# Order and place of small products on TensorE's array, in a two-layer hybrid encoder on one core

## The reference

```python
def retention_mixer(p, cos, sin):
    ...
    scores = jnp.einsum('bcqhd,bcshd->bchqs', q, k) * decay_mask
    o_inner = jnp.einsum('bchqs,bcshe->bcqhe', scores, v)
    ...
    o_cross = jnp.einsum('bcqhd,hq,bchde->bcqhe', q.astype(jnp.float32), q_decay, prev)
    o = (o_inner.astype(jnp.float32) + o_cross).reshape(B, -1, H, d)[:, pad:]

def rwkv7_mixer(p, v_first, vres, mu, w0, w_up, a0, a_up, g_up, k_k, k_a, r_k, gn_w, gn_b):
    ...
    w = w0 + jnp.tanh(wd) @ w_up                 # rank 32
    a = jax.nn.sigmoid(a0 + ad @ a_up)           # rank 32
    g = jax.nn.sigmoid(gd) @ g_up                # rank 64
    if vres is not None:                         # layer 1 only, rank 32
        v = v + (v_first - v) * jax.nn.sigmoid(v0 + (v @ v_down) @ v_up)
    ...
    def step(S, inp):                            # state S of 64 x 64 per head
        sa = jnp.einsum('bhvk,bhk->bhv', S, -kk_t)
        S = (S * w_t[:, :, None, :] + sa[..., None] * (kk_t * a_t)[:, :, None, :]
             + v_t[..., None] * k_t[:, :, None, :])
        return S, jnp.einsum('bhvk,bhk->bhv', S, r_t)
    ...
    y = group_norm_per_head(y); return (y + bonus) * g
```

## Time and profile before

| | |
|---|---|
| median of 3 runs | 3283.07 us |
| profiled execution, its time | 3285.28 us |
| profiled execution, its span | 3283.1 us |
| TensorE matmul busy | 3237.2 us (99%) |
| VectorE busy | 1343.1 us (41%) |
| ScalarE busy | 870.8 us (27%) |
| share of 16 DMA engines' span, weights' queue | 40.0% |
| mean granted TensorE clock | 0.998 |

### The profile page before, as it was taken

How to read it: one execution, slowest core, us unless ns; L and a number is a source line. 1 busy time by engine, 2 the same in 40 slices (tenths; PEclk the granted TensorE clock), 3 DMA queues, 4 the chain that set the end, 5 groups by cost and what they waited for, 6 DMA issues and landing times.

```text
span 3283.1 us, 51407 instructions
## 1 busy us (share of the span) xinstructions
PE 3237.2 (99%) x21648; PEld 2737.6 (83%) x21648; DVE 1343.1 (41%) x3184; ACT 870.8 (27%) x2565; POOL 34.2 (1%) x47
## 2 busy tenths in 40 slices
PE   8999999999999999999999999999999999999998
PEld 6788788888888888878888888888888888888887
DVE  4335451345514454153541544415354154442541
ACT  3323430224303242032430324204232042411320
POOL 0000000000000000000000000000000000000000
PEclk9999999999999999999999999999999999999999
DMA  6233234442444334443334433444334433345443
GB/s 202 70 120 123 97 123 145 145 134 98 135 151 148 126 101 145 154 135 123 109 117 152 138 128 98 148 151 138 118 119 151 159 130 116 123 149 165 149 154 115
DMA packets 128867, 434.79 MB, mean 132 GB/s; under 512 B 13296, under 2 KB 25712, under 8 KB 128384
## 3 DMA queue, kind: packets, MB, share of 16 engines
q1 hardware_dynamic: 127488, 427.32, 40.0%
q0 software_dynamic: 1152, 4.19, 0.3%
HBM read 427.27 MB, written 4.19 MB: 131 GB/s over the span
## 4 chain that ended last, share of the span: by engine, by line
PE 97%; DVE 1%; ACT 1%; issue 0%; DMA 0%; SPq 0%; POOL 0%; ACTq 0%; DVEq 0%
PE psum L859 66%; PE psum L1307 19%; PE psum L853 2%; PE psum L873 2%; PE psum L1107 1%; PE psum L1120 1%; PE psum L1064 1%; PE psum L1123 1%; PE psum L1140 1%; PE psum L1249 1%; PE psum L1232 0%; PE psum L1202 0%; PE psum L1205 0%; PE psum L1187 0%; DMA con<-in_consts 0%
## 5 line engine op out<-in xcount | busy, mean ns | idle before, releaser
L859 PE MATMUL psum<-hT,slots 128*128 128x256 f32 (+2 forms) x8832 | 1998.7, 384 | 10.7 <-DMA con<-in_consts 2.9
L859 PEld LDWEIGHTS psum<-hT,slots 128*128 128x128 f32 x8832 | 1661.4, 190 | 284.4 <-issue 38.6
L1307 PE MATMUL psum<-gT,slots 128*128 128x256 f32 (+1 forms) x2816 | 615.4, 381 | 0.3 <-DVE hT L1411 0.2
L1307 PEld LDWEIGHTS psum<-gT,slots 128*128 128x128 f32 x2816 | 533.9, 190 | 78.5 <-issue 0.5
L1411 DVE SCALAR_TENSOR_TENSOR hT<-hT,psum 128x256 f32<-128x256 f32 (+2 forms) x128 | 54.2, 424 | 617.4 <-PE psum L1307 504.8
L785 ACT ACTIVATE last<-psum 128x2 f32<-128x2 f32 x352 | 60.2, 171 | 904.3 <-PE psum L859 904.2
L859 PE MATMUL psum<-mixT,slots 128*128 128x256 f32 (+2 forms) x1024 | 227.1, 382 | 2.0 <-DVE hT L1411 1.7
L859 PEld LDWEIGHTS psum<-mixT,slots 128*128 128x128 f32 x1024 | 193.6, 190 | 34.3 <-issue 6.6
L1867 DVE TENSOR_SCALAR tmpG<-raw,par 128x256 f32<-128x256 f32 (+2 forms) x176 | 62.5, 355 | 380.0 <-ACT raw L786 379.7
L555 ACT ACTIVATE scr<-hT 128x256 f32<-128x256 f32 (+2 forms) x120 | 47.6, 419 | 587.8 <-DVE hT L1430 564.4
L1867 DVE TENSOR_SCALAR gT<-raw,par 128x256 f32<-128x256 f32 (+2 forms) x176 | 62.3, 354 | 327.5 <-ACT raw L786 327.4
(11 more groups left out here) (246 smaller groups left out, 2386.4 us busy)
## 6 DMA issues: line engine op xcount, KB each, us to landing
slots<-in_weights SPq DMA_DIRECT2D x792, 512.0 KB, 3.4
hT<-in_x SPq DMA_DIRECT2D x8, 512.0 KB, 5.4
out<-prpt POOLq DMA_DIRECT2D x8, 512.0 KB, 3.0
tab<-in_tables SPq DMA_DIRECT2D x6, 512.0 KB, 5.2
con<-in_consts SPq DMA_DIRECT2D x1, 1562.0 KB, 10.6
tab<-in_tables SPq DMA_DIRECT2D x2, 544.0 KB, 5.2
mixT<-in_ln_rows SPq DMA_DIRECT2D x1, 1024.0 KB, 7.0
par<-in_params SPq DMA_DIRECT2D x2, 386.5 KB, 5.5
```

Of the source, the lines that this page charges most:

```text
L859: ins = mm(psum[:, i % 2, :n], lhsT, rhs, start=k == 0, stop=k == len(pairs) - 1)
L1307: ins = mm(psum[:, i % 2, :n], w[:, e * P:(e + 1) * P], gT[:, k, first:first + n], start=k == 0, stop=k == KF - 1)
```

## The change

The low-rank products are issued `lw0`, `la0`, `lw1`, `la1`, `lg0`, `lg1`, and ScalarE reads them in that order. `lt` is computed with 128 output rows (the further columns of the stationary operand are whatever parameters lie behind `vdown`), and `lv0`, `lv1` with 128 input rows; rows 32 to 127 of `vup` are zero. Retention issues all four L1202 products of a tile, then all four L1205 products. RWKV outputs go by pairs of heads, and for odd heads in full tiles the two sub-chunks exchange their output rows, in L1005, L1008 and L1027. ScalarE puts them back in place when it reads the transposes, with three copies in place of one for each full tile.

```diff
-SMALL_BANK = dict(lw0=2, la0=3, lg0=4, lw1=5, la1=6, lg1=7, ss0=2, ss1=3, lt=4, lv0=5, lv1=6, bo0=2, bo1=3,
+SMALL_BANK = dict(lw0=2, la0=3, lw1=5, la1=6, lg0=4, lg1=7, ss0=2, ss1=3, lt=4, lv0=5, lv1=6, bo0=2, bo1=3,
...
-                        small(u, "lt", temp("lt", n), parts=32)
+                        small(u, "lt", temp("lt", n))
...
+                    y = bank(R0 + i)[:, 0:256].rearrange("p (t s) -> p t s", t=2)
+                    if j == 0:
+                        ins = act(mixT[:, 6:8, off:off + n], y[:, :, :n], ACT.Copy)
+                    else:
+                        act(mixT[0:HD, 6:8, off:off + n], y[0:HD], ACT.Copy)
+                        for cc in range(2):
+                            a0 = off + HD * (1 - cc)
+                            ins = act(mixT[HD:, 6:8, a0:a0 + HD], y[HD:, :, HD * cc:HD * cc + HD], ACT.Copy)
+                    ins.then_inc(S["w_yTc"], 1)
...
-                vdown = par[:, a + P_AT["vdown"]:a + P_AT["vdown"] + 64]
+                vdown = [par[:, a + P_AT["vdown"] + 32 * ct:a + P_AT["vdown"] + 32 * ct + P] for ct in range(2)]
...
-                        for ct in range(2):
-                            for tag, base, rank in (("lw", 0, 32), ("la", 32, 32), ("lg", 64, 64)):
+                        for ranks in ((("lw", 0, 32), ("la", 32, 32)), (("lg", 64, 64),)):
+                            for ct in range(2):
+                                for tag, base, rank in ranks:
...
-                        small(u, "lt", [(vdown[:, 32 * ct:32 * ct + 32], row(f"v{ct}", n)) for ct in range(2)], parts=32)
+                        small(u, "lt", [(vdown[ct], row(f"v{ct}", n)) for ct in range(2)])
...
-                            small(u, f"lv{ct}", [(vup[0:32, ct * P:(ct + 1) * P], temp("lt", n)[0:32])])
+                            small(u, f"lv{ct}", [(vup[:, ct * P:(ct + 1) * P], temp("lt", n))])
...
+                def to(h, cs):
+                    return slice(HD - cs.start, 2 * HD - cs.start) if h % 2 and j else cs
+                for ct in range(2):
+                    for h in (2 * ct, 2 * ct + 1):
+                        for cc, w, cs in chunks_in(n):
+                            mm(y_out(h)[to(h, cs)], S2[i][cs, h, 0, :w], Vt[i][cs, h * HD:(h + 1) * HD],
+                               start=h < 2, stop=False, skip_group_check=True)
+                    for h in (2 * ct, 2 * ct + 1):
+                        for cc, w, cs in chunks_in(n):
+                            ins = mm(y_out(h)[to(h, cs)], S1[cs, i, h, 0, :w], X[cs, i, h, HD:],
+                                     start=False, stop=j == 0, skip_group_check=True)
...
-                            ins = mm(y_out(h)[HD * cc:HD * cc + HD], ET[pb:pb + HD, ct, HD * cc:HD * cc + HD],
+                            ins = mm(y_out(h)[to(h, slice(HD * cc, HD * cc + HD))], ET[pb:pb + HD, ct, HD * cc:HD * cc + HD],
...
+                    for h in range(4):
+                        ins = mm(out_T(h), rVt[:n_, h * HD:(h + 1) * HD], rSM[:n_, h, :n_], start=h < 2, stop=j == 0,
+                                 skip_group_check=True)
+                    for h in range(4) if j else ():
+                        ct, pb = h // 2, HD * (h % 2)
+                        ins = mm(out_T(h), rS[pb:pb + HD, nth % 2, ct, :], row(f"qd{ct}", n_, off)[pb:pb + HD],
+                                 start=False, stop=True, skip_group_check=True)
```

More of the change, by code:

```diff
@@ L711, in rwkv @@
                     a.wait_ge(S["w_yT"], nth_tile(u, j) + 1)
-                    act(mixT[:, 6:8, off:off + n], bank(R0 + i)[:, 0:256].rearrange("p (t s) -> p t s", t=2)[:, :, :n],
-                        ACT.Copy).then_inc(S["w_yTc"], 1)
+                    y = bank(R0 + i)[:, 0:256].rearrange("p (t s) -> p t s", t=2)
[7 more added lines that the diff above has]
+                    ins.then_inc(S["w_yTc"], 1)
                 yield
@@ L931, in project @@
                         pe.wait_ge(S["lo_act"], 2 * u + 2)
-                        for ct in range(2):
-                            for tag, base, rank in (("lw", 0, 32), ("la", 32, 32), ("lg", 64, 64)):
-                                small(u, f"{tag}{ct}",
-                                      [(up[base:base + rank, ct * P:(ct + 1) * P], row("lo", n)[base:base + rank])])
+                        for ranks in ((("lw", 0, 32), ("la", 32, 32)), (("lg", 64, 64),)):
+                            for ct in range(2):
+                                for tag, base, rank in ranks:
+                                    small(u, f"{tag}{ct}",
+                                          [(up[base:base + rank, ct * P:(ct + 1) * P], row("lo", n)[base:base + rank])])
                     if i == 6:
```

## The result

The changed kernel takes 3264.26 us (median of 4 runs, 3264.09 to 3264.36) beside 3283.08 us for the kernel before (4 runs, 3282.22 to 3284.09): a ratio of 0.9941, 95% interval [0.9925, 0.9957]. In a larger sample the kernel before had a median of 3283.97 us (13 runs, 3282.14 to 3285.75), and in the one taken with the last experiment 3285.09 us (7 runs, 3282.22 to 3285.82), so the difference is 18.8 to 20.8 us by the sample. The forecast was 3262 with a range of 3258 to 3267.

What follows compares the result with a forecast made beforehand. TensorE, busy for 3237.2 of 3283.1 us, was taken to bound the kernel. Savings of 3.1 + 2.8 + 4.8 + 7.5 + 3.0 = 21.2 us, subtracted from the median of 3283.07, gave 3262 us, range 3258 to 3267.

Steps and rivals of the forecast that it cites:

- A: Low-rank products: reordering leaves two changes of tile shape instead of four, 0.19 us each in 8 units, 3.1 us saved.
- B: `lt` and `lv`, widened to full size, cost no change of shape: 0.70 us in 4 units, 2.8 us saved.
- C: Retention outputs: two runs in 1.17 us instead of four in 1.47, 0.30 in 16 tiles, 4.8 us saved.
- D: RWKV outputs L1005 and L1008: crossing fills four quadrants, four runs instead of eight, 0.467 in 16 tiles, 7.5 us saved.
- The first rival: Row halves exclude each other in a PSUM bank, so the RWKV outputs gain nothing: 3269.4 us, chance 0.07.
- The second rival: The extra belongs to products, not shape changes; low-rank, `lt`/`lv` and retention gains don't come: 3272.6 us, chance 0.05.
- The third: Crossed quadrants exclude each other at RWKV outputs and state products, so the kernel gets slower: 3294.8 us, chance 0.03.
- the fourth: Nothing moves, since another engine or the weights' transfers take over: about 3283 us, chance 0.02.
- E: State's products L1022 and L1027: the exchange relieves the fullest quadrant in sub-chunk 1, 0.19 in 16 tiles, 3.0 us saved.
- a third fall of the clock: TensorE's clock, seen falling twice at 1.7 us each, might fall once more, giving 3264 us.
- F: ScalarE's three copies add 0.9 us for two tiles; slack of 2.5 us in unit 0 makes that cost nothing.

Runs made afterwards that it cites:

- e1: The changed kernel with odd heads' RWKV outputs back in their own output rows, still issued by pairs, and ScalarE's copy one again: 3272.5 us.
- e2: The changed kernel with ScalarE taking, in each round, the retention and attention step ahead of the RWKV step: 3264.31 us.
- e5: The kernel of e4 with ScalarE's retention and attention step ahead of its RWKV step from unit 3 on only: 3248.78 us.
- e4: The changed kernel with half of the triangular inverse's (tile, head) pairs keeping their own row half, to fill all four quadrants: 3252.21 us.
- e3: The kernel before with only the RWKV outputs' pairing and crossing and ScalarE's three copies: 3275.02 us.

## Why the prediction was right

**A, B, C, D.** Right in mechanism and in size. By the starts of records, A gives 0.39 in each of 8 units (3.15 us; forecast 3.1), B 0.70 in each of 4 (2.8; 2.8), C 0.30 in each of 16 tiles (4.8; 4.8), D 0.467 in each of 16 tiles (7.5; 7.5). Each was made from starts of records at a place in the kernel with the same shapes. The waits of unit 0 did not take in what A and C save there, as had seemed possible: the lead is 1.0 us ahead of the first fall of the clock and 1.0 behind it.

**The rule of the PSUM bank.** Four records in a slot with both row halves in one bank do run side by side: 32 records of L1020 and L1024 take 0.577 us to the dense tile. Nor is there time for the row halves to take turns: at the dense tile's pace, 0.216 us for 256 columns, 64 columns need 0.054 us (an estimate) of the slot's 0.058. The first rival (0.07) is refuted. The Trainium skill, "TensorEngine Tiling (Array Packing)", section on gotchas (PSUM pressure), says without exception that different row tiles can't access one bank at the same time; the trace does not agree where the two row halves write different partition halves of the bank. No run here tries two row halves on the same partitions of a bank.

**The extra per change of shape.** The second rival (0.05) is refuted by the retention block: two L1217 pairs in a row hold one extra, 0.58 for what would be 0.73 in two runs. The third (0.03) and the fourth (0.02) fall with D: with crossed quadrants the output block takes 0.57 us instead of 1.04, and the kernel is faster.

**E.** The blocks gave 0.207 a tile for the second sub-chunk, less 0.007 for the first: 3.2 us, forecast 3.0. But the step "a microsecond that TensorE doesn't spend at a place where it does not wait is a microsecond of the kernel" was not checked behind the block: I looked for what waits at the place, and not for how much room the next wait had. There it was 0.1 us, and TensorE came 0.47 earlier by D. The five waits took back 2.1 us. That the time still fell into the range was in part luck: its upper end had room for E at 0 and for a third fall of the clock, and none was meant for waits. e1 shows that they come with the crossing, e2 and e5 that they go when ScalarE's exponentials no longer stand behind the copy of F.

**F.** Right: VectorE's last step in unit 0 ends at 208.1 and TensorE's product behind that wait starts at 209.59, so the room fell from 2.5 to 1.5 us.

```profile
204.39 0.38 ACT L717 ACTIVATE mixT<-psum 64x256 f32<-64x256 f32 x1 [0.17 <-PE psum L861]
204.78 0.44 ACT L720 ACTIVATE mixT<-psum 64x128 f32<-64x128 f32 x2
205.24 0.38 ACT L717 ACTIVATE mixT<-psum 64x256 f32<-64x256 f32 x1
205.62 0.44 ACT L720 ACTIVATE mixT<-psum 64x128 f32<-64x128 f32 x2
```

A tile's three copies take 0.85 us from start to start; I had said 0.75.

**The sum.** Blocks 21.4, less 2.1 for five waits and 0.1 for a smaller one in unit 1, is 19.2; the timed medians differ by 18.8 and, with the larger sample of before, by 19.7. The forecast's 21.2 misses by the waits, 2.2 us that it put at nothing. In the profiled runs the last TensorE record is 20.9 us earlier: 19.2 by the blocks and waits, 1.6 because one of the two clock falls is gone, and 0.1 from the start. That the spans so differ by almost the forecast 21.2 is chance.

**The clock.** A stretch at the place of the second fall, in the changed kernel, whose profiled run lacks it (start and end, length, busy time and records of PE, PEld, DVE, ACT and POOL, granted clock, DMA share, GB/s):

```profile
3022.00:3030.00 8.00, 5.61 (x27) 4.64 (x26) 2.74 (x7) 2.12 (x7) 0.00 (x0) 1.00 0.27 73
```

The same place in e1, where it is there, a granted clock of 0.66 over 5 us:

```profile
3032.00:3037.00 5.00, 3.77 (x10) 3.12 (x11) 1.47 (x4) 0.51 (x2) 0.00 (x0) 0.66 0.26 103
```

The wait of TensorE is 2.39 us in both, so it does not decide by itself whether the clock falls. The kernel before and e4 had the fall in their profiled runs, and e2, e3 and e5 did not. What decides it stays open. Some of the spread between runs of one kernel (3282.1 to 3285.8 for the one before) may be this; that was not settled, since the timed runs list only a mean clock of 0.997 to 0.999.

## What to carry to other kernels

On an engine that is busy throughout, price an edit by the starts of records at a place of the same shape, and count quadrants: here a block of 64x64 products cost about as many slots of 0.058 us as its fullest quadrant had records, and every change of tile shape between blocks 0.15 to 0.2 us. Look then for the next wait behind each shortened block and measure its room: here 0.1 us of room met 0.47 us of gain, five times. Padding a small operand to full size cost TensorE nothing between full-size products: `lt` and `lv` pass at the pace of the dense tiles.

## What the runs showed of the hardware

- Products to a free quadrant started ahead of earlier products to busy ones: L1043 pairs start 0.03 us behind L1038 pairs, with six records of L1038 still to come.
- Two row halves wrote one PSUM bank, on different partition halves, at the full pace: eight records of L1020 or L1024 in 0.117 us, four in 0.058.
- Full-size float32 products passed at 0.216 us a record for 256 columns whether they belong to a dense tile or stand four by four between two.
- One change of the tile's shape less saved 0.197 us at the low-rank products (128 output rows; 0.394 for two) and 0.149 us at the retention outputs (64 output rows; 0.298 for two).
